# Experts wholly in two-part form in twelve parts of 1024 columns, two first chunks side by side, the prompt's softmax beside the last gates, nineteen late modulation items

## What is computed

```python
mod = silu(cond) @ mod_w + mod_b            # six vectors: sh1, sc1, g1, sh2, sc2, g2
h = rms_norm(x, norm1_w) * (1 + sc1) + sh1
hy, qkv, scv, gates = split(h @ w_in)       # 1536, 768, 1536, 3072 columns
ya = hyena_mixer(...)                       # long convolution, here by Fourier tables
yb = blocked_gqa(q, k, v)                   # 8 heads of 64, 2 key heads; prompt sees prompt only
yc = bgate * conv3(cgate * u)
merged = sum(sigmoid(gate) * (y @ w_br))    # three branches
x = x + g1 * (merged @ w_o)
h2 = rms_norm(x, norm2_w) * (1 + sc2) + sh2
aff = softmax(h2 @ router_w); gate, idx = top_k(aff.T, 2 * N / 16)   # 16 experts, 16 + 64 rows each
x = x + g2 * scatter_add(gate * ((silu(xs @ w_gate) * (xs @ w_up)) @ w_down))
```

## Time and profile before

| | |
|---|---|
| three runs | 2358.04 us median (2357.45 to 2365.32) |
| the profiled execution | 2358.94 us, its span 2357.2 us |
| PE busy | 2219.6 us (94%), mean granted clock 0.967 |
| DVE, ACT, POOL busy | 1390.8, 1001.1, 168.5 us |
| DMA | 436.21 MB, mean 185 GB/s; nine tenths and more busy only in the expert stages |

### The profile page before, as it was taken

One profiled execution on the slowest core, in us unless ns is written; L12 is line 12 of the kernel. 1 busy time (PEld: TensorE's weight loads), 2 busy tenths in 40 slices (PEclk: granted clock), 3 DMA queues, 4 the chain that ended last, 5 costly groups with the idle time before them and its releaser, 6 DMA issues.

```text
span 2357.2 us, 38875 instructions
## 1 busy us (share of the span) xinstructions
PE 2219.6 (94%) x14664; PEld 1886.8 (80%) x14664; DVE 1390.8 (59%) x2271; ACT 1001.1 (42%) x1792; POOL 168.5 (7%) x224
## 2 busy tenths in 40 slices
PE   7998999999888998899998999999897999699999
PEld 3447999999656996688886999999763999488887
DVE  5855432511767555688887453431467654688887
ACT  2433212232622223688875311222460222588885
POOL 0010000010100100111110000001100110011110
PEclk8999999999998998899999999999998999799999
DMA  9782221333322524999992112233501331799995
GB/s 371 261 304 80 72 72 72 116 120 116 126 74 94 165 83 160 383 382 381 385 390 80 72 72 72 89 116 120 185 5 45 132 132 54 284 386 388 384 378 202
DMA packets 72960, 436.21 MB, mean 185 GB/s; under 512 B 9289, under 2 KB 9929, under 8 KB 31930
## 3 DMA queue, kind: packets, MB, share of 16 engines
q1 hardware_dynamic: 46368, 331.89, 36.8%
q0 software_dynamic: 22160, 88.61, 11.6%
q10 hardware_dynamic: 4300, 13.90, 1.7%
HBM read 384.87 MB, written 49.50 MB: 184 GB/s over the span
## 4 chain that ended last, share of the span: by engine, by line
PE 82%; DVE 8%; DMA 3%; ACT 2%; issue 2%; DVEq 2%; ACTq 0%; POOL 0%; POOLq 0%
PE ps L633 39%; PE ps L1102 8%; PE ps L1132 7%; PE ps L1090 5%; PE ps L1106 4%; PE ps L814 4%; PE ps L732 2%; PE ps L714 2%; PE ps L864 1%; PE ps L672 1%; PE ps L966 1%; DMA front<-kspec 1%; DVE back L1919 1%; DVE nb L1880 1%; DMA ring<-in_stream 1%
## 5 line engine op out<-in xcount | busy, mean ns | idle before, releaser
L633 PE MATMUL ps<-front_r 128*128 128x320 f32 x5888 | 932.9, 311 | 27.8 <-DVE front_r L1606 13.5
L633 PEld LDWEIGHTS ps<-front_r 128*128 128x128 f32 x5888 | 883.8, 189 | 34.8 <-issue 11.0
L1590 DVE TENSOR_TENSOR front_r<-ring,front_r 128x1024 fp32r<-128x1024 f32 x148 | 181.2, 1225 | 475.6 <-ACT front_r L1199 474.5
L1199 ACT ACTIVATE front_r<-ring 128x1024 fp32r<-128x1024 f32 (+1 forms) x180 | 176.4, 980 | 381.9 <-PE ps L633 291.7
L1199 ACT ACTIVATE back<-ps 128x512 f32<-128x512 f32 (+5 forms) x240 | 113.1, 496 | 403.4 <-PE ps L633 165.7
L1102 PE MATMUL ps<-back_r 128*80 128x256 f32 x640 | 171.8, 291 | 0.0
L1102 PE MATMUL ps<-back_r,front_r 128*80 128x256 f32 x640 | 164.2, 279 | 0.0
L2069 DVE TENSOR_TENSOR back_r<-front,back_r 128x512 fp32r<-128x512 f32 x208 | 137.7, 687 | 26.9 <-ACT back_r L1199 25.0
L1132 PE MATMUL ps<-back_r,front_r 128*80 128x512 f32 x576 | 149.6, 395 | 0.0
L633 PE MATMUL ps<-back_r,front_r 128*128 128x320 f32 x640 | 148.2, 313 | 0.0
L1359 ACT ACTIVATE back<-ps 128x640 f32<-128x640 f32 x48 | 33.9, 706 | 232.0 <-PE ps L633 231.9
(11 more groups left out here) (246 smaller groups left out, 3198.2 us busy)
## 6 DMA issues: line engine op xcount, KB each, us to landing
ring<-in_stream SPq DMA_DIRECT2D x186, 1024.0 KB, 7.4
front<-in_stream SPq DMA_DIRECT2D x80, 1024.0 KB, 14.9
back<-in_stream SPq DMA_DIRECT2D x48, 1024.0 KB, 15.3
gates<-back POOLq DMA_DIRECT2D x48, 320.0 KB, 2.4
back<-gates POOLq DMA_DIRECT2D x48, 320.0 KB, 3.3
kspec<-back POOLq DMA_DIRECT2D x20, 512.0 KB, 7.2
front<-kspec POOLq DMA_DIRECT2D x4, 2048.0 KB, 11.5
rows<-front ACTq DMA_DIRECT2D x10, 520.0 KB, 3.0
```

The lines of the kernel that those rows point to most:

```text
L633: mm = pe.matmul(tokh(b)[:, c0:c1], w(wp)[:, k, :], src(hp, k)[:, c0:c1], start=first, stop=last)
L1199: return act.activation(o, i, ACT.Copy)
L1590: dve.tensor_tensor(half_dst(u, 1), src, half_dst(u, 0).bitcast(F32), ALU.subtract).then_inc(w_lo, 1)
```

## The change

1. Modulation items: 29 ahead of the layers instead of 32; 19 late ones instead of 16: in layer 0 five in the convolution (two and three) and four beside top-k, in layer 1 six (two and four) and four.
2. The first two chunks of each input projection run side by side: both work through h as its eighths come, chunk 1 four eighths behind. The first transposes come right after them.
3. Between the two norm products of layer 1, `keep_busy(1, 4)` goes. The two first splits of layer 1 are made by ACT and DVE ahead of the sum of the experts instead of after the root. An unread square root stands ahead of ACT's wait for each root.
4. The prompt's scores come between the last two groups of gate chunks, its softmax beside the last gates, in PSUM; after the last chunk only the product with the reciprocal sum is left, which DVE makes before the row maximum of the first block.
5. Experts: gate and up of one half of the hidden columns stand side by side in two items, so that the whole first matmul is 8 parts of 1024 columns with 48 fp32r products of 512 columns; the down projection is 4 parts. ACT and DVE make 12 parts instead of 20 quarters, in 4 places of 1024 columns. The plain fp32 gate and its copy of the rows go. In the last expert `load_sum` stands before parts 9, 10 and 11 (three at once).

```diff
-MODS, LATE = DEPTH * N_MOD, (4, 8, 4)
-EARLY = MODS - sum(LATE)
+MODS, LATE = DEPTH * N_MOD, ((5, 4), (6, 4))
+EARLY = MODS - sum(sum(n) for n in LATE)
...
-        W5 = [region_r(kb, [2, 512]) for kb in (56, 60, 64, 68, 41)]
-        NQ5, UPQ = 5, 12
+        W4 = [region_r(kb, [2, 1024]) for kb in (56, 64, 40, 125.25)]
+        NW, UPH = 4, 8
...
-            return (6 + n,) if n < 14 else (2 * n - 8, 2 * n - 7)
+            return (6 + n,) if n < 17 else (2 * n - 11, 2 * n - 10)
+        def conv_mods(l, o):
+            return late_mods(l, 0)[2:] if o else late_mods(l, 0)[:2]
...
                     mean_squares(l, 0)
-                    keep_busy(1, 4)
                     spread(l, 0)
                     keep_busy(1, 6)
...
+                def first_chunks(lag):
+                    def tile(c, k):
+                        for wp, hp in ((0, 0), (0, 1), (1, 0)):
+                            for c0, c1 in HALVES:
+                                mm = pe.matmul(tokh(c)[:, c0:c1], w2(c, KC, wp)[:, k, :], h_part(hp, k)[:, c0:c1],
+                                               start=k + wp + hp == 0, stop=k == KC - 1 and wp == 1)
+                        if k == KC - 1:
+                            mm.then_inc(chunk_ready, 1)
+                    half_ready(l, 0)
+                    for k in range(KC + lag):
+                        if k < KC:
+                            pe.wait_ge(x_lo, l * OP + k + 1)
+                            tile(0, k)
+                        if k == lag:
+                            half_ready(l, 1)
+                        if k >= lag:
+                            tile(1, k - lag)
+                first_chunks(4)
+                transposes(0)
+                for c in range(2, 24):
...
-                with pe.Fori(4, 6) as it:
-                    gate_chunks(it)
+                gate_chunks(4)
                 pe.wait_ge(a_trev, l * 6 + 6)
+                for j in range(4):
+                    for g in range(2):
+                        mm = pe.matmul(ps[:, 4 + g, P * j:P * j + P], qT[head(g), j, 0:P], kT[head(g), 0:P],
+                                       start=True, stop=True)
+                mm.then_inc(p_s, 1)
+                gate_chunks(5)
...
-                    if l == 0:
-                        pe.wait_ge(y_odd, 3 * o + 3)
-                        for i in conv_mods(o):
+                    pe.wait_ge(y_odd, l * 6 + 3 * o + 3)
+                    for i in conv_mods(l, o):
...
+                        def up(v):
+                            hf, k0 = v // 4, 2 * v % KC
+                            hi, lo = (place_of(ee, v)[:, i, :].rearrange("p (k n) -> p k n", k=2) for i in range(2))
+                            pe.wait_ge(e_whi, part(l, b, ee, v + 1))
+                            for k in range(2):
+                                for x in (xe_hi, xe_lo):
+                                    pe.matmul(ps[0:SLOTS, hf, :], x[:, k0 + k, :], hi[:, k, :],
+                                              start=k0 + k == 0 and x is xe_hi, stop=False)
+                            pe.wait_ge(e_wlo, part(l, b, ee, v + 1))
+                            for k in range(2):
+                                mm = pe.matmul(ps[0:SLOTS, hf, :], xe_hi[:, k0 + k, :], lo[:, k, :], start=False,
+                                               stop=k0 + k == KC - 1)
+                                if k == 0 and v % 2:
+                                    mm.then_inc(item_used, 1)
+                            mm.then_inc(e_used, 1)
...
-                        pe.wait_ge(e_x, l * NE + b * 4 + ee + 1)
-                        first_gate()
                         pe.wait_ge(e_xlo, l * NE + b * 4 + ee + 1)
-                        up(1)
-                        up(2)
+                        for v in range(6):
+                            up(v)
                         turn_hidden(0)
-                        up(3)
+                        up(6)
+                        up(7)
...
+                        down(8)
                         if not last or ee < 3:
                             turn_rows((ee + 1) % 4, b * 16 + (l * 64 + 16 * ((ee + 1) // 4) + 16))
+                        turn_hidden(1)
+                        down(9)
+                        pe.wait_ge(e_hlo, l * 2 * NE + b * 8 + 2 * ee + 2)
+                        down(10)
+                        down(11)
...
+                        if last and n == 4:
+                            act.wait_ge(p_sub, l + 1)
+                            act.activation(ps[:, 4:6, :], ps[:, 4:6, :], ACT.Exp).then_inc(p_exp, 1)
...
+                        for v in range(3, 7):
+                            part_hi(b, ee, v)
                         silu(0)
+                        part_hi(b, ee, 7)
+                        part_hi(b, ee, 8)
                         hidden_hi(0)
+                        for v in range(9, 12):
                             if last and ee == 3:
-                                load_sum(v - 13)
+                                for t in ((0,), (1,), (2, 3, 4))[v - 9]:
+                                    load_sum(t)
+                            if v == 11:
+                                silu(1)
+                            part_hi(b, ee, v)
+                        if follows:
+                            part_hi(b, ee + 1, 0)
                         hidden_hi(1)
+                        if follows:
                             evac_rows(b * 4 + (l * NE + ee + 2))
+                            part_hi(b, ee + 1, 1)
+                            part_hi(b, ee + 1, 2)
...
                 rows = Pp.rearrange("p g (j n) -> p (g j) n", j=4)
+                dve.wait_ge(chunk_ready, (l + 1) * CHUNKS)
                 settle()
+                dve.tensor_tensor(rows, found, pst[:, 2, :].unsqueeze(2).to_broadcast([P, 8, P]),
+                                  ALU.mult).then_inc(p_norm, 1)
                 row_max(0)
```

More of the change, by code:

```diff
@@ L798, in _ @@
                         wait_chunk_freed(pe, l, c - 3)
-                    wait = (lambda k: pe.wait_ge(x_lo, l * OP + k + 1)) if c == 0 else None
-                    chunk(c % 3, lambda part: w2(c, KC, part), h_part, KC, wait).then_inc(chunk_ready, 1)
-                    if 1 <= c <= 8:
+                    chunk(c % 3, lambda part: w2(c, KC, part), h_part, KC).then_inc(chunk_ready, 1)
+                    if c <= 8:
                         transposes(c - 1)
@@ L896, in values @@
                     mm.then_inc(a_vals, 1)
-                for j in range(4):
-                    for g in range(2):
-                        mm = pe.matmul(ps[:, 4 + g, P * j:P * j + P], qT[head(g), j, 0:P], kT[head(g), 0:P],
-                                       start=True, stop=True)
-                mm.then_inc(p_s, 1)
                 scores(0)
@@ L1220, in root @@
             def root(l, n):
+                act.activation(unread[:], eps[:, 0:1], ACT.Sqrt)
                 act.wait_ge(s_ms, l * 2 + n + 1)
@@ L2207, in weight_stream @@
             for hf in range(2):
-                columns(o[p + 2 * hf:], w["exp_w_gate"][l, e][:, 256 * hf:256 * hf + 256], 256, KC)
-                columns(o[p + 2 * hf + 1:], w["exp_w_up"][l, e][:, 256 * hf:256 * hf + 256], 256, KC)
+                both = np.concatenate([w[name][l, e][:, 256 * hf:256 * hf + 256] for name in ("exp_w_gate", "exp_w_up")], 1)
+                for kh in range(2):
+                    columns(o[p + 2 * hf + kh:], both[512 * kh:512 * kh + 512], 512, 4)
             columns(o[p + 4:], w["exp_w_down"][l, e], 512, 4)
```

289 lines of the change are left out of this document (118 added, 171 removed).

## The result

The changed kernel ran in 2317.8 us (median; 2314.85 to 2319.68), the kernel before beside it in 2357.75; the ratio is 0.9825, with a 95% interval from 0.9809 to 0.9841. Run again beside the experiments it took 2316.0 us (2313.86 to 2321.33) against 2358.9. The forecast was 2316, with a range from 2303 to 2331. The profiled execution took 2319.68 us with a span of 2318.0, against a span of 2357.2 before.

What follows compares the result with a forecast made beforehand. The prediction took PE as the bound, only just ahead of DVE and DMA in the experts. Terms sum to 42.2 us: 2358.9 - 42.2 - 0.9 = 2315.8, stated as 2316, with 8 in 10 for 2303 to 2331.

Steps and rivals of the forecast that it cites:

- three items fewer in the filters: Filters: each item costs PE 1.28 us with no gap around it, so three fewer gain 3.8 us.
- late items in the convolution: Convolution, both layers: the added items fit into PE's standing time, so cost 0, bound 2 us.
- router to experts, layer 0: Four items instead of eight make layer 0 like layer 1; 7.85 us less a lower-clock first gate, net 7.1 (6 to 8).
- prompt's softmax: Between last gates and second scores: 3.85 us less waiting plus 1.26 from the clock, 5.1 a layer, 10.2 (7 to 12).
- first two chunks: Start of each input projection: transposes then wait for DVE's convolution of chunk 0; 1.3 us a layer, 2.6 (0 to 5.3).
- norm of layer 1: Norm before layer 1: the spread starts about 2.6 us earlier but at the lower clock; 1.4 us gained (0 to 2.6).
- experts, layer 0: Experts of layer 0: DMA's queue sets the layer's end, at 287.7 us; 6.8 us gained.
- experts, layer 1: Experts of layer 1: PE sets the pace at 17.46 us an expert, ending at 284.2 us; 10.3 us gained.
- DMA binds nowhere: Rival, experts: DMA never limits, layer 0 gains as layer 1; 2310 us, or 2304 with further gains; chance 0.17.
- it binds from the start: Rival, experts: DMA limits throughout, 18.12 us an expert, 1.6 us a layer gained instead of 8.5; 2330 us; chance 0.14.
- The slower case: Rival, experts: DVE binds, still standing 2.99 us, so 20.0 us an expert; 2388 us; chance 0.04.
- the third rival: Between the stages: gate chunks wait for softmax work; half of 14.2 us (softmax, norm, first chunks) lost; 2323 us; chance 0.10.

Runs made afterwards that it cites:

- u_filters: Changed kernel with three late modulation items put back into the filters (sixteen late instead of nineteen); 2319.07 us, ratio 0.9824 to the kernel before.
- u_router: Changed kernel with eight items instead of four between router and experts of layer 0, fewer in the convolutions; 2325.98 us, ratio 0.9854 to the kernel before.
- u_softmax: Changed kernel with the prompt's softmax behind the last gates again; 2326.65 us, ratio 0.9869 to the kernel before.
- u_chunks: Changed kernel with the first two chunks one behind the other again; 2317.48 us, ratio 0.982 to the kernel before.
- k_conv: Kernel before, plus idle PE products in layer 1's convolution (16 in the first order, 32 in the second); 2364.16 us, ratio 1.0018 to the kernel before.
- s_sums: Changed kernel with the loads of the sums issued by SP, behind the next layer's four ring loads, instead of by ACT; 2315.96 us, ratio 0.9818.
- l_light: s_sums with each replacing load of an expert's item bringing only 1536 of its 2048 columns; 2306.15 us, ratio 0.978 to the kernel before.

## Why the prediction was right

The total was right, 42.2 forecast against 40.0 and 42.9 by the two pairs of medians, and so were the mechanisms of the largest terms. That it came out so close is in part luck: the convolution and layer 1's experts gave 1 to 2 us each more than forecast, the first chunks 1.1 less, the router in one pair 3.6 less, and these misses cancel.

| Term | forecast | shown by the stretches |
|---|---|---|
| three items fewer in the filters | 3.8 | 4.3, 3.7 to 4.8 (u_filters) |
| late items in the convolution | 0 | 1.2 to 2.2 in layer 1; none shown in layer 0 |
| router to experts, layer 0 | 7.1 | 7.3 and 3.5 in the two pairs of traces; 6 to 7 by u_router |
| prompt's softmax | 10.2 | 10.8 (u_softmax) |
| first two chunks | 2.6 | 1.5 (u_chunks) |
| norm of layer 1 | 1.4 | 0.2 in the pair, 0.2 to 1.9 over all traces; not isolated |
| experts, layer 0 | 6.8 | 6.1 and 8.9 in the two pairs |
| experts, layer 1 | 10.3 | 11.7 and 12.3 in the two pairs |

**Filters.** Right in kind. In the pair of profiles the gain doesn't show, since the start of the execution after took 4.1 us more; that it isn't the change's doing is shown by the kernel before with 56.31 us.

**Convolution: the step that failed.** "All are covered", cost 0, bound 2 as a loss only. The items are covered, but the cover was read one-sidedly: PE's stand of 9.74 us had a price behind it: the four products after it take 3.78 us where such four take 1.88 at the full clock. I had charged that price at the softmax and at the first expert and forgot it here. k_conv shows it without any item: 2.6 us. In layer 0 nothing is shown: with five items the stretch takes 84.1 to 85.8 us, and with four, as before, 84.6 to 85.9.

**Router.** Right in kind; the size is less sure than the pair of profiles makes it. The same code of before took 52.94 us in one trace and 50.09 in k_conv, 1.85 of the difference before the first late item, where the granted clock was 0.66 (915:925) against 1.00 in k_conv (917:927). The second part is right too: the experts do start at the lower clock. In the chain of the kernel after the first four products of layer 0 take twice what the same four take an expert later:

```profile
945.25 1.99 PE ps L1119 x4
...
965.02 0.93 PE ps L1119 x4
```

**Softmax.** Right in both steps. The second scores come 3.95 us after the first and not 5.0, and the clock kept up behind them (1.6 a layer up to the convolution). The two loads of function tables that the rows didn't price took 1.28 us each and the exponential 1.01, and PE has no gap beside them. DVE's and ACT's waits among the splits held nobody up: from the first chunk to the first scores the kernel after has 399.93 and 399.92 us against 399.43 in the quiet execution of before, which is the 1.0 of the 16 products less 0.65 of the chunks. The profiled execution of before had 401.05 in layer 0, that of after 401.20 in layer 1; why these had 1.4 to 1.6 more is open.

**First two chunks.** The mechanism is right: the transposes wait for DVE's convolution (1.18 us at L795). The size was off, 0.7 and 0.8 us instead of 1.3. The forecast let chunk 0 end when it always had, and counted from there. But tiles of chunk 1 now stand between its own. The chain of the kernel after, layer 1:

```profile
1267.88 6.61 PE ps L804 x42
```

Chunk 0 ends with it, at 1274.49, 13.58 us after its first product (1260.91); before it ended at 1299.65 - 7.05 = 1292.60, 13.10 after its first product (1279.50). These 0.5 us are missing from the 1.3.

**Norm of layer 1.** No run takes this part of the change back, so the term stays open. The stretch from the sums to layer 1's first chunk took 27.4 and 27.9 us before and 26.0 to 27.2 in the traces that leave the place as changed; with the sums at SP it took 27.90 again, at a granted clock of 0.76 and without any change of this code. The clock that the end of the experts leaves behind moves it as much as the whole term.

**Experts, loop.** 17.37 us against 17.46 forecast; no gap, DVE at 97%, both as written. The margin of DVE, called the weakest point at 0.5, measured 0.36 to 0.44. ACT's work was sized at 13 us and is 14.77, since a part takes it 1.05 us and not 0.98; that cost nothing here. The one thing not forecast is the turn of the loop, with its two loads of function tables: 1.09 us at two turns of each layer, 2.2 us a layer. Before, the same two loads stood 1.9 us apart and PE had no gap. The faster loop made them count, and the 0.09 us an expert that the loop is shorter than forecast pays for 1.4 of the 2.2. In layer 1 the forecast had 284.2 and the trace 283.7; a part of that is two errors that cancel. The gain of 10.3 was counted from layer 0's 294.5, but layer 1 took 295.4 before: from its own length the same 284.2 is 11.2, and this is most of what the table shows as missed.

**Experts, DMA.** The queue grows as forecast. The end of layer 0 came as forecast too, after 288.5 and 287.4 us against 287.7; the 0.5 us between that and its own 287.2 have no reason in the forecast. Ring loads in layer 0, windows 965:1000 and 1141:1176, to be held beside the earlier trace rows:

```profile
ring<-in_stream SPq DMA_DIRECT2D x4, 1024.0 KB, 15.8
...
ring<-in_stream SPq DMA_DIRECT2D x4, 1024.0 KB, 22.8
```

That is 7.0 us in ten experts, 0.70 each where the forecast had 0.66. By the rates of the Trainium skill (HBM Reference, section Specifications (TRN2): 425 GB/s for a core alone) the queue would have drained, since an expert's 7.0 MB would need 16.5 us, an estimate, and an expert takes 17.37. At 385 GB/s with full share it doesn't drain; with a quarter of the bytes left out it stays short, 7.1 us in the first of these windows and 7.2 in the second. At the end of layer 0 the forecast had PE waiting for the sums. In the kernel after the wait takes another form. The chain of the two layers' ends:

```profile
1213.10 9.26 DMA acc<-back,idx
...
2293.03 8.04 DMA back<-acc
```

ACT stands 3.66 us for the landing of the last scatter, where the forecast allowed 0 to 2.3, DVE and PE stand behind it, and by the time PE asks for the sums they are there. The size is about the same, since the same queue sets both: s_sums turned it back into 4.99 us at the sums, and l_light took all but 1.05 of it away. In layer 1, where no loads of a next layer follow, the last scatter lands after 5.23 us instead of 9.26, ACT doesn't stand for it, and PE waits 1.53 us for the sums, as forecast (1 to 3).

**The rivals.** That DMA binds nowhere is ruled out by l_light, that it binds from the start by 17.37 us an expert in both. The slower case, DVE's standing of 2.99 us that stays, is ruled out by the same 17.37, in which DVE stands about 0.5. Between the stages a part of the gain was nearly half lost, as the third rival had it (the chunks), but the softmax was whole.

## What to carry to other kernels

Price a stand of PE twice, for its length and for the products behind it: work that moves into it can gain, though it was only meant to be hidden there. Where a loop becomes faster, look again at what was hidden in it at no cost, such as loads of function tables at its head. And where a transfer queue is full, moving a wait to another engine changed here who stands and not how long; only fewer bytes did.

## What was not expected of the hardware

- The same code took 52.2 to 56.4 us to the fourth product of the filters, with the granted clock between 50 and 60 us at 0.73 to 1.00, and 152.9 to 156.6 us between branches and router. The values come in groups (52.2, 53.0 to 54.1 and 56.3 to 56.4 us for the first); what chooses between them is open.
- In the midst of the experts a scatter or a gather lands after 8.8 to 10.6 us by the medians in the windows 965:1000 and 1141:1176, whether ring loads in the same engines take 7.2 us (l_light) or 23.1 (s_sums). In these runs it was quicker where few or no loads were left beside it: the last scatter of layer 0 took 8.79 us in s_sums and 5.41 in l_light, that of layer 1 4.92 and 5.20.
- One product of 128 x 256 with float32 operands is two instructions of 0.21 us, 0.43 us in all at the full clock. Read as one, it made two experiments overrun.
